# Dilated attention on one Trainium2 core: reordering softmax maxima and sums between token orders by VectorE transposes and quadrant copies instead of TensorE table products

## The chip, the cores and the metric

The kernel runs on one core of one Trainium2 chip. The metric is the device time of one execution in microseconds (us), as the median of several runs. Less is better.

## The reference

One decoder layer: a half-step feed-forward block, a mixer with two attention branches, and a second half-step feed-forward block, for 512 tokens and a model width of 1024. The change touches the dilated branch alone. It has three groups of eight heads; group 0 attends to a window of neighbours (stride 1), groups 1 and 2 to tokens 4 and 16 apart. The three groups of one head index are mixed by weights that come from their softmax maxima and sums:

```
m = jnp.max(logits, axis=-1, keepdims=True)
p = jnp.exp(logits - m)
den = jnp.sum(p, axis=-1, keepdims=True)
out = jnp.einsum('brnhqk,brnkhd->brnqhd', (p / den).astype(v.dtype), vv)
lse = (m + jnp.log(den))[..., 0]
...
w = jax.nn.softmax(jnp.stack(lses, axis=0), axis=0)
y = jnp.sum(w[..., None] * jnp.stack(outs, axis=0).astype(jnp.float32), axis=0)
```

For one token, `w` needs the maxima and sums of all three groups. Group 0 is computed with 128 consecutive tokens on the 128 partitions (token = 128b + p); groups 1 and 2 with every fourth token (token = 4p + b). So each group's maxima and sums must also be had in the other token order before the weights can be formed in both.

## The kernel before

All products are made on TensorE (PE) in three passes of high and low parts (`act_hi*w_hi`, `act_lo*w_hi`, `act_hi*w_lo`). The weights stream in as pieces: SyncE (SP) loads a piece into one of four `raw` buffers, ScalarE (ACT) rounds it to `w_hi` (`split_hi`), VectorE (DVE) subtracts to get `w_lo` (`split_lo`, semaphore `lo_ready`), and PE multiplies 24 matmuls per whole piece. Two buffers of `w_hi` and `w_lo` exist, so ACT splits a piece only once PE is done with the one two before.

The dilated part handles two heads of each group at a time: `dilated_pair`, four turns (the first written out, three in a loop). Each turn has pieces q = 0 to 11: q 0 to 5 give queries and keys of the three groups, 6 to 8 the values, 9 and the half pieces 10 and 11 two output gates. Each engine has its own program in written order and waits on semaphores:

- PE: `dil_project(q)`, with scores (`dil_score`) after pieces 2, 4 and 6, value transposes (`turn_dil_values`) after 7, 8 and 9, then transposes of the probabilities (`turn_dil`) and the products with values (`attend_dil`) in and between the half pieces. `turn_dil_values(2)` after piece 9 needs VectorE's taking of piece 8 (semaphore `chunk_taken`); `turn_dil(0)` needs the probabilities of group 0 scaled by their weights (`scale_probs(0)`, `dil_scaled`).
- VectorE: `split_lo` of the next piece, `dil_maxima` (after pieces 3, 5, 7), `take_projection` (multiplying PE's result by `rstd`), and at q = 9 `group_weights`, `scale_probs` and `gate_take`.
- ScalarE: `split_hi`, the exponentials, which leave each row's sum in `stats`, one small exponential in the middle of `group_weights`, and copies of transposed values and probabilities out of PSUM.

`stats` has 128 partitions x 2 (maxima, sums) x 3 groups x 2 token orders x 8. The other order is produced by PE: after `turn_dil_values(1)` it multiplies `stats` by 0/1 tables in `const` (`C_FOLD` and `C_EXPAND`, 512 columns each), four products each, into bank 7 (lines L827 and L830). `group_weights` on VectorE waits for them (`stats_moved`), masks the result with two more small tables (L1551) and adds up with twelve reductions (L1559, L1562).

Of the kernel before, what the change touches and what calls it, by code (L numbers as in the profile page):

```python
# [28 lines left out]
ALU = mybir.AluOpType  # L29
# [94 lines left out]
LATENTS = (KQ, KQ + 1, 0, 1, 2, None)  # L124


C_IDENT, C_ONES, C_EXPAND, C_FOLD = 0, P, 2 * P, 2 * P + SEQ
C_MOD = C_FOLD + SEQ
C_DIV = C_MOD + BLOCKS
C_CAUSAL = C_DIV + BLOCKS  # L130
C_FREQ = C_CAUSAL + P
C_TURN, C_PHASE, C_SIGN, C_EPS = C_FREQ + 1, C_FREQ + 2, C_FREQ + 3, C_FREQ + 4
C_END = C_FREQ + 5
# [26 lines left out]
def shape_constants():  # L160

    c = np.zeros((P, C_END), np.float32)
    p = np.arange(P)
    j = np.arange(SEQ)
    c[:, C_IDENT:C_IDENT + P] = np.eye(P)
    c[:, C_ONES:C_ONES + P] = 1.0

    c[:, C_EXPAND:C_EXPAND + SEQ] = p[:, None] == j[None, :] // 4
    c[:, C_MOD:C_MOD + BLOCKS] = p[:, None] % 4 == np.arange(4)

    c[:, C_FOLD:C_FOLD + SEQ] = p[:, None] == (4 * (j % P) + j // P)[None, :] % P
    c[:, C_DIV:C_DIV + BLOCKS] = p[:, None] // 32 == np.arange(4)
    c[:, C_CAUSAL:C_CAUSAL + P] = np.where(p[None, :] <= p[:, None], 0.0, NEG_INF)

    freq = 1.0 / ROPE_THETA ** (np.arange(0, QK_ROPE, 2, dtype=np.float32) / np.float32(QK_ROPE))
    for row in range(QK_NOPE, P):
        c[row, C_FREQ] = freq.astype(np.float32)[row % 16]
        cosine = row < QK_DIM
        c[row, C_TURN] = 0.25 if cosine else 0.0
        c[row, C_PHASE] = math.pi / 2 if cosine else 0.0  # L180
        c[row, C_SIGN] = -1.0 if QK_DIM <= row < QK_DIM + 16 else 1.0
    c[:, C_EPS] = EPS
    onehot = np.zeros((NUM_BUCKETS, T5_END), np.float32)
    mask = np.full((GROUP_HEADS, T5_END), NEG_INF, np.float32)
    for g, stride in enumerate(STRIDES):
        apart = (T5_LEN[g] + 1) // 2 + (P // 2 if g == 0 else 0) - 1 - np.arange(T5_LEN[g])
        unit = 4 if g == 2 else 1
        ok = (apart >= 0) & (apart <= P) & (apart % unit == 0)
        bucket = t5_bucket(np.maximum(apart, 0) // unit * stride)
        at = T5_AT[g] + np.arange(T5_LEN[g])  # L190
        onehot[bucket[ok], at[ok]] = 1.0
        mask[:, at[ok]] = 0.0
    return c, onehot, mask


def decoder_layer(nc, x_t, positions, rel_bias, gains_in, tables, onehot_in, mask_in, ffn, w_latent, w_lora_up,
# [19 lines left out]
    def sem(name):  # L216
        return ctx.enter_context(nc.semaphore(name))

    with ctx:
# [30 lines left out]

        exchanged = work[:, 3, 0:6 * 4 * 2 * BLOCKS]


        hid_hi = shared("hid_hi", [P, KF, SEQ], F32R)
# [79 lines left out]
        dil_scores, dil_taken = sem("dil_scores"), sem("dil_taken")  # L336
        dil_max, dil_exp, dil_scaled = sem("dil_max"), sem("dil_exp"), sem("dil_scaled")
        v_turned, v_taken = sem("v_turned"), sem("v_taken")
        stats_moved, weight_ready, weight_exp = sem("stats_moved"), sem("weight_ready"), sem("weight_exp")

        mixed_rounded, mixed_split = sem("mixed_rounded"), sem("mixed_split")
        merge_ready, merged_rounded, merged_split = sem("merge_ready"), sem("merged_rounded"), sem("merged_split")
# [151 lines left out]
        def _(pe):  # L494
# [283 lines left out]
            def dilated_pair(i, first=False):  # L778
# [43 lines left out]
                pe.wait_ge(chunk_taken, c + e + 8)  # L822
                turn_dil_values(1, i)

                pe.wait_ge(dil_exp, 24 * i + 24)
                for b in range(BLOCKS):
                    nc.tensor.matmul(bank[7][:, b * 16:(b + 1) * 16], const[:, C_FOLD + b * P:C_FOLD + (b + 1) * P],  # L827
                                     stats[:, :, 0, 0, :], start=True, stop=True, skip_group_check=True)
                for b in range(BLOCKS):
                    last = nc.tensor.matmul(bank[7][:, 64 + b * 32:96 + b * 32],  # L830
                                            const[:, C_EXPAND + b * P:C_EXPAND + (b + 1) * P],
                                            stats[:, :, 1:3, 1, :], start=True, stop=True, skip_group_check=True)
                last.then_inc(stats_moved, 1)
                dil_project(9)
                pe.wait_ge(chunk_taken, c + e + 9)
                turn_dil_values(2, i)
# [40 lines left out]
        def _(act):  # L877
# [209 lines left out]
            def dilated_pair(i, first=False):  # L1087
                s, d, c, e = PIECES["dil"], 12 * i, CHUNKS["dil"], 11 * i
                for q in range(10):
                    if q or not first:  # L1090
                        split_hi(act, s + q + 1, d, HALF if q == 9 else TILES)
                    if q == 0 and not first:

                        gate_tanh(c + e - 1, MLA_HEADS - 1 + 2 * i)
                    if q in (3, 5, 7):
                        dil_exponentials(q // 2 - 1, i)
                    if q in (7, 8):
                        take_dil_values(q - 7, i)

                act.wait_ge(weight_ready, i + 1)  # L1100
                nc.scalar.activation(weight[:, :, :], weight[:, :, :], ACT.Exp).then_inc(weight_exp, 1)
                take_dil_values(2, i)
                split_hi(act, s + 11, d, HALF)
                for unit in range(8):
                    take_dil_probs(unit, i)
                    if unit == 1:
                        gate_tanh(c + e + 9, MLA_HEADS + 2 * i)
                    if unit == 4:
                        split_hi(act, s + 12, d, TILES)
# [34 lines left out]
        def _(dve):  # L1144
# [3 lines left out]
            def one():  # L1148
                count["turn"] += 1
                return 1  # L1150

            def so_far():
                return count["before"] + count["turn"] + count["earlier"]
# [384 lines left out]
            def take_projection(out, s, d, parity):  # L1538
                dve.wait_ge(piece_done, s + d + 1)
                nc.vector.tensor_tensor(out, bank[parity][:, :], rstd[:, :], ALU.mult).then_inc(chunk_taken, 1)  # L1540

            def group_weights(i):

                dve.wait_ge(stats_moved, i + 1)
                moved = exchanged
                mod, div = const[:, C_MOD:C_MOD + BLOCKS], const[:, C_DIV:C_DIV + BLOCKS]

                for at, n, mask in ((0, 8, div), (64, 16, mod)):
                    size = n * 8
                    view = "p (r k e) -> p r k e"  # L1550
                    nc.vector.tensor_tensor(  # L1551
                        moved[:, at:at + size].rearrange(view, k=BLOCKS, e=2),
                        bank[7][:, at:at + size].rearrange(view, k=BLOCKS, e=2),
                        mask.rearrange("p (a k e) -> p a k e", a=1, e=1).to_broadcast([P, n, BLOCKS, 2]), ALU.mult).then_inc(own, one())
                dve.wait_ge(own, so_far())
                for t in range(2):
                    for e in range(2):
                        source = moved[:, 0:64].rearrange("p (a t k e) -> p t e a k", a=BLOCKS, t=2, e=2)[:, t, e]
                        nc.vector.tensor_reduce(stats[:, t, 0, 1, e:8:2], source, AX.X, ALU.add)  # L1559
                        for g in (1, 2):  # L1560
                            source = moved[:, 64:192].rearrange("p (b t g k e) -> p t g e b k", b=BLOCKS, t=2, g=2, e=2)
                            last = nc.vector.tensor_reduce(stats[:, t, g, 0, e:8:2], source[:, t, g - 1, e], AX.X, ALU.add)  # L1562
                last.then_inc(own, one())
                dve.wait_ge(own, so_far())
                maxima_of = stats[:, 0, :, :, :].rearrange("p g o n -> p g (o n)")
                sums_of = stats[:, 1, :, :, :].rearrange("p g o n -> p g (o n)")
# [4 lines left out]
                top = neg_top[:, :].rearrange("p (a n) -> p a n", a=1).to_broadcast([P, GROUPS, 4 * BLOCKS])  # L1571
                nc.vector.tensor_tensor(weight[:, :, :], top, maxima_of, ALU.subtract).then_inc(weight_ready, 1)
                dve.wait_ge(weight_exp, i + 1)
                parts = exchanged[:, 0:GROUPS * 4 * BLOCKS]
                nc.vector.tensor_tensor(parts.rearrange("p (g n) -> p g n", g=GROUPS), weight[:, :, :],
                                                    sums_of, ALU.mult).then_inc(own, one())
                dve.wait_ge(own, so_far())
# [18 lines left out]
            def dilated_pair(i, first=False):  # L1596
                s, d, c, e = PIECES["dil"], 12 * i, CHUNKS["dil"], 11 * i
                for q in range(12):
                    tiles = HALF if q in (9, 10) else TILES
                    if q or not first:  # L1600
                        split_lo(dve, s + q + 1, d, tiles)
                    if q in (3, 5, 7):
                        dil_maxima(q // 2 - 1, i)
                    if q < 6:
                        out = (dil_q, dil_k)[q % 2][:, q // 2, :]
                    else:
                        out = dil_vt[:, q % 2, :]
                    if q == 0 and not first:

                        take_mixed(PAIRS - 1 + i, PAIRS + 8 * i, bank[2][:, :])  # L1610
                    if q < 9:
                        take_projection(out, s + q, d, (c + q) % 2)
                    if q == 9:
                        group_weights(i)
                        scale_probs(0)
                        gate_take(s + d + 10, (c + 9) % 2, MLA_HEADS + 2 * i)
                        for g in (1, 2):
                            scale_probs(g)
                gate_take(s + d + 12, 4, MLA_HEADS + 2 * i + 1)
            dilated_pair(0, first=True)  # L1620
            with dve.Fori(1, PAIRS) as i:
                enter_loop(i - 1, 2 + 1 + 2 + 4)
                dilated_pair(i)
            leave_loop(PAIRS - 1)

# [122 lines left out]
```

## Time and profile before

| | us |
|---|---|
| median of 3 runs | 1312.73 |
| lowest and highest run | 1310.87, 1315.46 |
| the profiled execution's own time | 1314.23 |
| its span, first to last instruction | 1312.4 |

| engine | busy us | share of the span |
|---|---|---|
| PE matmul | 1290.6 | 98% |
| PE weight load | 1048.9 | 80% |
| DVE | 653.1 | 50% |
| ACT | 443.0 | 34% |
| POOL | 18.7 | 1% |

The mean granted TensorE clock is 0.996 of full speed. Matmuls are pipelined, so PE's busy time is a union of overlapping records; the distance between the starts of two matmuls says more of what one costs than its duration. The four turns of the dilated part lie at about 545 to 860 us.

### The profile page before, as it was taken

What the parts mean: (1) busy time and instruction counts of PE and PEld (TensorE: products, weight loads), DVE (VectorE), ACT (ScalarE), POOL (GpSimd) and SP (SyncE); (2) the same over time, 40 slices, a digit from 0 to 9 for tenths busy, and PEclk for the clock granted to TensorE, in tenths of its full rate; (3) what the DMA queues carried; (4) which work ended last, traced back from release to release, by engine and by line L of the source; (5) the groups of instructions that cost most, each with busy time, mean ns of one, the idle gap of its engine ahead of it and who ended that gap; (6) DMA issues with size and microseconds to landing.
All of it is one profiled execution on the core that took longest, in us unless ns stands there. A gap on an engine that the chain in (4) does not pass through costs nothing.

```text
span 1312.4 us, 16722 instructions
## 1 busy us (share of the span) xinstructions
PE 1290.6 (98%) x6054; PEld 1048.9 (80%) x6054; DVE 653.1 (50%) x943; ACT 443.0 (34%) x763; POOL 18.7 (1%) x36
## 2 busy tenths in 40 slices
PE   8999999999999999999999999999999999999997
PEld 6788888888887777788888878778888888888886
DVE  5644444433345777544554545576644444443322
ACT  5322222322232444343333334423432222222221
POOL 0000000000000001200000000000000000000000
PEclk9999999999999999999999999999999999999998
DMA  6242232233321112512222221123222222223331
GB/s 224 97 110 96 96 96 96 88 104 89 104 90 62 67 54 79 130 50 82 78 65 86 74 80 64 64 96 96 97 96 96 96 96 96 96 90 91 100 88 64
DMA packets 36066, 118.87 MB, mean 91 GB/s; under 512 B 4680, under 2 KB 4680, under 8 KB 36032
## 3 DMA queue, kind: packets, MB, share of 16 engines
q1 hardware_dynamic: 34416, 114.83, 27.2%
q0 software_dynamic: 1328, 3.56, 1.5%
q8 instruction: 20, 0.33, 0.1%
q14 instruction: 14, 0.11, 0.0%
q10 hardware_dynamic: 288, 0.03, 0.0%
HBM read 115.85 MB, written 2.55 MB: 90 GB/s over the span
## 4 chain that ended last, share of the span: by engine, by line
PE 93%; DVE 3%; ACT 1%; issue 1%; DMA 1%; SPq 0%; POOL 0%; POOLq 0%; ACTq 0%; DVEq 0%
PE bank L545 36%; PE bank L378 17%; PE bank L380 16%; PE bank L379 16%; PE bank L732 2%; PE bank L755 1%; PE bank L649 1%; ACT w_hi L360 1%; PE bank L676 1%; DVE mla_stats L1441 1%; PE bank L665 1%; PE bank L772 1%; PE bank L768 1%; PE bank L512 0%; PE bank L741 0%
## 5 line engine op out<-in xcount | busy, mean ns | idle before, releaser
L365 DVE TENSOR_TENSOR w_lo<-raw,w_hi 128x1024 fp32r<-128x1024 f32 (+2 forms) x221 | 259.1, 1172 | 252.9 <-ACT w_hi L360 251.2
L360 ACT ACTIVATE w_hi<-raw 128x1024 fp32r<-128x1024 f32 (+2 forms) x221 | 224.3, 1015 | 446.7 <-PE bank L545 230.4
L545 PE MATMUL bank<-act_hi,w_hi 128*128 128x512 f32 x704 | 218.4, 391 | 2.8 <-DVE act_lo L1165 2.8
L545 PE MATMUL bank<-act_lo,w_hi 128*128 128x512 f32 x704 | 216.8, 389 | 0.0
L545 PE MATMUL bank<-act_hi,w_lo 128*128 128x512 f32 x704 | 216.6, 389 | 0.0
L378 PE MATMUL bank<-act_hi,w_hi 128*128 128x512 f32 x528 | 212.7, 403 | 2.9 <-DVE mla_vt L1434 1.5
L380 PE MATMUL bank<-act_hi,w_lo 128*128 128x512 f32 x528 | 206.7, 391 | 0.0
L379 PE MATMUL bank<-act_lo,w_hi 128*128 128x512 f32 x528 | 206.5, 391 | 0.0
L545 PEld LDWEIGHTS bank<-act_hi,w_hi 128*128 128x128 f32 x704 | 132.1, 188 | 32.2 <-DVE w_lo L365 3.2
L545 PEld LDWEIGHTS bank<-act_lo,w_hi 128*128 128x128 f32 x704 | 132.1, 188 | 27.7
L545 PEld LDWEIGHTS bank<-act_hi,w_lo 128*128 128x128 f32 x704 | 132.1, 188 | 27.5
L378 PE MATMUL bank<-hid_hi,w_hi 128*128 128x512 f32 x352 | 136.9, 389 | 0.0
L379 PE MATMUL bank<-hid_lo,w_hi 128*128 128x512 f32 x352 | 136.9, 389 | 0.0
L380 PE MATMUL bank<-hid_hi,w_lo 128*128 128x512 f32 x352 | 136.9, 389 | 0.0
L378 PEld LDWEIGHTS bank<-act_hi,w_hi 128*128 128x128 f32 x528 | 99.5, 188 | 29.6 <-issue 6.5
L380 PEld LDWEIGHTS bank<-act_hi,w_lo 128*128 128x128 f32 x528 | 99.5, 188 | 21.8
L379 PEld LDWEIGHTS bank<-act_lo,w_hi 128*128 128x128 f32 x528 | 99.7, 189 | 18.7
L1250 DVE TENSOR_TENSOR work<-bank,rstd 128x512 f32<-128x512 f32 x44 | 30.4, 692 | 123.3 <-PE bank L545 123.2
L380 PEld LDWEIGHTS bank<-hid_hi,w_lo 128*128 128x128 f32 x352 | 66.1, 188 | 13.8
L379 PEld LDWEIGHTS bank<-hid_lo,w_hi 128*128 128x128 f32 x352 | 66.1, 188 | 13.7
L378 PEld LDWEIGHTS bank<-hid_hi,w_hi 128*128 128x128 f32 x352 | 66.1, 188 | 13.6
L925 ACT ACTIVATE hid_hi<-work 128x512 f32 (+1 forms) x44 | 27.8, 632 | 94.8 <-DVE work L1256 94.8
(173 smaller groups left out, 1070.1 us busy)
## 6 DMA issues: line engine op xcount, KB each, us to landing
raw<-in_ffn_up SPq DMA_DIRECT2D x87, 512.0 KB, 3.4
raw<-in_w_dil SPq DMA_DIRECT2D x40, 512.0 KB, 3.4
raw<-in_ffn_down SPq DMA_DIRECT2D x32, 448.0 KB, 3.3
raw<-in_ffn_down SPq DMA_DIRECT2D x16, 512.0 KB, 3.5
raw<-in_w_mla_gates SPq DMA_DIRECT2D x8, 512.0 KB, 3.5
raw<-in_w_branches SPq DMA_DIRECT2D x8, 512.0 KB, 3.4
raw<-in_w_out SPq DMA_DIRECT2D x8, 512.0 KB, 3.4
raw<-in_w_latent SPq DMA_DIRECT2D x6, 512.0 KB, 3.5
```

The costliest lines, as they stand in the source:

```text
L360: nc.scalar.activation(w_hi[:, s % SPLIT, 0:tiles * P], raw[:, s % RAW, 0:tiles * P], ACT.Copy).then_inc(hi_ready, 1)
L365: nc.vector.tensor_tensor(w_lo[:, s % SPLIT, 0:tiles * P], raw[:, s % RAW, 0:tiles * P], w_hi[:, s % SPLIT, 0:tiles * P].bitcast(F32), ALU ...
L378: nc.tensor.matmul(out, a, hi(k), start=first, stop=False)
L379: nc.tensor.matmul(out, a, lo(k), start=False, stop=False)
L380: last = nc.tensor.matmul(out, b, hi(k), start=False, stop=end)
L545: last = nc.tensor.matmul(out, w[:, s % SPLIT, tile * P:(tile + 1) * P], moving[:, row, :], start=row == 0 and w is w_hi and moving is act_hi,
L649: nc.tensor.matmul(out, mla_q[0:QK_DIM, h % 2, b * P:(b + 1) * P], mla_k[0:QK_DIM, h % 2, 0:(b + 1) * P], start=True, stop=False, skip_gro ...
L665: last = nc.tensor.transpose(bank[5 + unit % 2][:, at:at + P], mla_p[:, row * P:(row + 1) * P], ident)
L676: last = nc.tensor.matmul(bank[7][V_DIM * e:V_DIM * (e + 1), key * P:SEQ], mla_v[:, e, key, :], probs_t[:, e, at:at + width], start=key == ...
L732: last = nc.tensor.matmul(out, dil_q[rows, g, tokens(g, b)], dil_k[rows, g, keys], start=True, stop=True, skip_group_check=True)
L925: nc.scalar.activation(hid_hi[:, bass.ds(2 * i + 2 * turn + j, 1), :], work[:, 3:4, :], ACT.Copy).then_inc(hid_rounded, 1)
L1250: nc.vector.tensor_tensor(work[:, 0, :], bank[c % UP_BANKS][:, :], rstd[:, :], ALU.mult).then_inc(chunk_taken, 1)
```

## The change

The eight table products per turn, their tables and the masks and reductions behind them go. Two VectorE functions take their place. Both use that a 32x32 transpose works within blocks of 32 partitions, and that a copy may move data from one quadrant (32 partitions) to another:

- `fold_stats` (at q = 5) brings group 0's maxima and sums into the order of groups 1 and 2: a transpose, four copies that gather the quadrants, a transpose, four copies that spread them.
- `expand_stats` (at q = 8) brings groups 1 and 2 into group 0's order: eight copies, a transpose, four copies, a transpose.
- On VectorE `group_weights` and `scale_probs(0)` move from q = 9 to q = 8, ahead of the taking of piece 8. On ScalarE the small exponential moves ahead of the copy of the second values.
- The table that is loaded at the start has 389 columns in place of 1421.

```diff
-C_IDENT, C_ONES, C_EXPAND, C_FOLD = 0, P, 2 * P, 2 * P + SEQ
-C_MOD = C_FOLD + SEQ
-C_DIV = C_MOD + BLOCKS
-C_CAUSAL = C_DIV + BLOCKS
+C_IDENT, C_ONES, C_CAUSAL = 0, P, 2 * P
...
-                pe.wait_ge(dil_exp, 24 * i + 24)
-                for b in range(BLOCKS):
-                    nc.tensor.matmul(bank[7][:, b * 16:(b + 1) * 16], const[:, C_FOLD + b * P:C_FOLD + (b + 1) * P],
-                                     stats[:, :, 0, 0, :], start=True, stop=True, skip_group_check=True)
-                for b in range(BLOCKS):
-                    last = nc.tensor.matmul(bank[7][:, 64 + b * 32:96 + b * 32],
-                                            const[:, C_EXPAND + b * P:C_EXPAND + (b + 1) * P],
-                                            stats[:, :, 1:3, 1, :], start=True, stop=True, skip_group_check=True)
-                last.then_inc(stats_moved, 1)
                 dil_project(9)
...
+                    if q == 8:
+
+                        act.wait_ge(weight_ready, i + 1)
+                        nc.scalar.activation(weight[:, :, :], weight[:, :, :], ACT.Exp).then_inc(weight_exp, 1)
                     if q in (7, 8):
                         take_dil_values(q - 7, i)
 
-                act.wait_ge(weight_ready, i + 1)
-                nc.scalar.activation(weight[:, :, :], weight[:, :, :], ACT.Exp).then_inc(weight_exp, 1)
                 take_dil_values(2, i)
...
+            def fold_stats(i):
+
+                dve.wait_ge(dil_exp, 24 * i + 8)
+                dve.wait_ge(own, so_far())
+                nc.vector.transpose(squares, stats[:, :, 0, :, :].rearrange("p t o n -> p t (o n)")).then_inc(own, one())
+                dve.wait_ge(own, so_far())
+                for u in range(BLOCKS):
+                    last = nc.vector.tensor_copy(by_stat[:, :, 8 * u:8 * u + 8],
+                                                 squares[SQ * u:SQ * (u + 1), :].rearrange("i (q v) -> i v q", v=BLOCKS))
+                last.then_inc(own, one())
+                dve.wait_ge(own, so_far())
+                nc.vector.transpose(by_token, work[0:SQ, 3, 4 * SQ:8 * SQ]).then_inc(own, one())
+                dve.wait_ge(own, so_far())
+                for b in range(BLOCKS):
+                    source = by_token.rearrange("q (v t n) -> q t v n", v=BLOCKS, t=2)[:, :, :, 2 * b:2 * b + 2]
+                    last = nc.vector.tensor_copy(
+                        stats[SQ * b:SQ * (b + 1), :, 0, 1, :].rearrange("q t (v e) -> q t v e", e=2), source)
+                last.then_inc(own, one())
+
+            def expand_stats(i):
+
+                dve.wait_ge(dil_exp, 24 * i + 24)
+                dve.wait_ge(own, so_far())
+                for b in range(BLOCKS):
+                    for t in range(2):
+                        target = by_token.rearrange("q (v t g b e) -> q b t g v e", v=BLOCKS, b=BLOCKS, t=2, g=2)
+                        last = nc.vector.tensor_copy(
+                            target[:, b, t], stats[SQ * b:SQ * (b + 1), t, 1:3, 1, :].rearrange("q g (v e) -> q g v e", e=2))
+                last.then_inc(own, one())
+                dve.wait_ge(own, so_far())
+                nc.vector.transpose(work[0:SQ, 3, 4 * SQ:8 * SQ], by_token).then_inc(own, one())
+                dve.wait_ge(own, so_far())
+                for u in range(BLOCKS):
+                    last = nc.vector.tensor_copy(squares[SQ * u:SQ * (u + 1), :].rearrange("i (q v) -> i v q", v=BLOCKS),
+                                                 by_stat[:, :, 8 * u:8 * u + 8])
+                last.then_inc(own, one())
+                dve.wait_ge(own, so_far())
+                nc.vector.transpose(stats[:, :, 1:3, 0, :], squares).then_inc(own, one())
+
             def group_weights(i):
 
-                dve.wait_ge(stats_moved, i + 1)
...
                     tiles = HALF if q in (9, 10) else TILES
+                    if q == 8:
+                        expand_stats(i)
                     if q or not first:
                         split_lo(dve, s + q + 1, d, tiles)
                     if q in (3, 5, 7):
                         dil_maxima(q // 2 - 1, i)
+                    if q == 5:
+                        fold_stats(i)
+                    if q == 8:
+                        group_weights(i)
+                        scale_probs(0)
...
                     if q == 9:
-                        group_weights(i)
-                        scale_probs(0)
                         gate_take(s + d + 10, (c + 9) % 2, MLA_HEADS + 2 * i)
                         for g in (1, 2):
                             scale_probs(g)
                 gate_take(s + d + 12, 4, MLA_HEADS + 2 * i + 1)
+            nc.vector.memset(stats[:, :, 0, 1, :], 0.0).then_inc(own, one())
```

The place on PE is the seam between pieces 8 and 9 of the first turn. Before, PE's program reads there (L741 is the transpose of values, L827 and L830 the table products, L378 to L380 the three passes of a piece):

```order
L380 MATMUL bank<-act_hi,w_lo 128x512
L741 MATMUL bank<-const,dil_vt 128x128 [waits v_taken,chunk_taken]
L741 MATMUL bank<-const,dil_vt 128x128 x3
L827 MATMUL bank<-stats,const 128x16 [waits dil_exp]
L827 MATMUL bank<-stats,const 128x16 x3
L830 MATMUL bank<-stats,const 128x32 x4
L378 MATMUL bank<-act_hi,w_hi 128x512 [waits lo_ready,chunk_taken]
```

And with the change (line numbers are five lower):

```order
L375 MATMUL bank<-act_hi,w_lo 128x512
L736 MATMUL bank<-const,dil_vt 128x128 [waits v_taken,chunk_taken]
L736 MATMUL bank<-const,dil_vt 128x128 x3
L373 MATMUL bank<-act_hi,w_hi 128x512 [waits lo_ready,chunk_taken]
L374 MATMUL bank<-act_lo,w_hi 128x512
```

Eight products and a wait on `dil_exp` are gone; the first product of piece 9 follows the value transposes.

On VectorE the place is from the taking of piece 7 to the splitting of the half piece 10, in the first turn. Before (L1540 takes a piece, L365 is `split_lo`, L1551 masks):

```order
L1540 TENSOR_TENSOR dil_vt<-bank,rstd 128x512 [waits piece_done]
L365 TENSOR_TENSOR w_lo<-raw,w_hi 128x1024 [waits hi_ready]
L1540 TENSOR_TENSOR dil_vt<-bank,rstd 128x512 [waits piece_done]
L365 TENSOR_TENSOR w_lo<-raw,w_hi 128x512 [waits hi_ready]
L1551 TENSOR_TENSOR work<-bank,const 128x64 [waits stats_moved]
L1551 TENSOR_TENSOR work<-bank,const 128x128
L1559 TENSOR_REDUCE stats<-work 128x4 [waits own]
```

With the change, from the same taking of piece 7 (L1528) to the first instruction of `group_weights` (L1574):

```order
L1528 TENSOR_TENSOR dil_vt<-bank,rstd 128x512 [waits piece_done]
L1556 COPY work<-stats 32x2x4x2 [waits own,dil_exp]
L1556 COPY work<-stats 32x2x4x2 x7
L1560 STREAM_TRANSPOSE work<-work 32x128 [waits own]
L1563 COPY work<-work 32x4x8 [waits own]
L1563 COPY work<-work 32x4x8 x3
L1567 STREAM_TRANSPOSE stats<-work 128x2x2x8 [waits own]
L360 TENSOR_TENSOR w_lo<-raw,w_hi 128x1024 [waits hi_ready]
L1574 TENSOR_TENSOR neg_top<-stats 128x16 [waits own]
```

and further on, the end of `group_weights` (L1589), `scale_probs(0)` (L1599), and only then the taking of piece 8 and the splitting for piece 10:

```order
L1589 TENSOR_TENSOR weight<-weight,total 128x48 [waits own]
L1599 TENSOR_TENSOR dil_p<-dil_p,weight 128x128 [waits own]
L1599 TENSOR_TENSOR dil_p<-dil_p,weight 128x768
L1599 TENSOR_TENSOR dil_p<-dil_p,weight 128x128
L1599 TENSOR_TENSOR dil_p<-dil_p,weight 128x768
L1528 TENSOR_TENSOR dil_vt<-bank,rstd 128x512 [waits piece_done]
L360 TENSOR_TENSOR w_lo<-raw,w_hi 128x512 [waits hi_ready]
```

Fourteen small instructions now stand ahead of the splitting for piece 9, and the weights and the scaling of group 0 ahead of the taking of piece 8. `fold_stats` puts ten more at q = 5, between `dil_maxima(1)` and the taking of piece 5.

## Rows read from the trace of the kernel before

**Rows 1.** The page: busy time of PE, and the granted clock in 40 slices

```profile
PE 1290.6 (98%) x6054; PEld 1048.9 (80%) x6054; DVE 653.1 (50%) x943; ACT 443.0 (34%) x763; POOL 18.7 (1%) x36
...
PEclk9999999999999999999999999999999999999998
```

**Rows 2.** Waits of PE: us in total, times, longest us

```profile
PE bank L545 <- DVE act_lo L1165: 2.8, 1, 2.8
...
PE bank L772 <- ACT probs_t L1085: 1.3, 4, 0.3
```

**Rows 3.** PE's timeline, first turn, pieces 8 to 9: start us, length us

```profile
591.70 0.63 PE L741 MATMUL bank<-const,dil_vt 128*128 128x128 f32 x4
592.17 0.96 PE L827 MATMUL bank<-stats,const 128*128 128x16 f32 x8
592.99 1.06 PE L830 MATMUL bank<-stats,const 128*128 128x32 f32 x8
593.88 0.48 PE L378 MATMUL bank<-act_hi,w_hi 128*128 128x512 f32 x1
```

**Rows 4.** PE's timeline, first turn, pieces 7 to 8

```profile
585.77 0.60 PE L741 MATMUL bank<-const,dil_vt 128*128 128x128 f32 x4
586.12 0.48 PE L378 MATMUL bank<-act_hi,w_hi 128*128 128x512 f32 x1
```

**Rows 5.** The tile `stats`: the table products, count, ns, first and last start

```profile
L827 PE MATMUL bank<-stats,const x32: 182/262/263, 592.2 to 828.0; 128*128 128x16 f32 x32
```

**Rows 6.** PE's timeline, last turn, pieces 8 to 9

```profile
826.78 0.63 PE L741 MATMUL bank<-const,dil_vt 128*128 128x128 f32 x4
...
828.96 0.48 PE L378 MATMUL bank<-act_hi,w_hi 128*128 128x512 f32 x1
```

**Rows 7.** VectorE's timeline, first turn, q = 7 to 9

```profile
585.97 0.69 DVE L1540 TENSOR_TENSOR dil_vt<-bank,rstd 128x512 f32<-128x512 f32 x1 [2.83 <-PE bank L380]
587.98 1.23 DVE L365 TENSOR_TENSOR w_lo<-raw,w_hi 128x1024 fp32r<-128x1024 f32 x1 [1.32 <-ACT w_hi L360]
...
593.52 0.69 DVE L365 TENSOR_TENSOR w_lo<-raw,w_hi 128x512 fp32r<-128x512 f32 x1 [0.93 <-ACT w_hi L360]
...
595.28 0.16 DVE L1559 TENSOR_REDUCE stats<-work 128x4 f32<-128x16 f32 x1
595.36 0.23 DVE L1562 TENSOR_REDUCE stats<-work 128x4 f32<-128x16 f32 x2
595.63 0.17 DVE L1567 TENSOR_TENSOR neg_top<-stats 128x16 f32<-128x16 f32 x1
595.84 0.17 DVE L1569 TENSOR_TENSOR neg_top<-neg_top,stats 128x16 f32<-128x16 f32 x1
...
597.58 2.23 DVE L1593 TENSOR_TENSOR dil_p<-dil_p,weight 128x128 f32<-128x128 f32 x4
```

**Rows 8.** ScalarE's timeline, first turn, q = 7 to 9

```profile
584.86 0.19 ACT L1073 ACTIVATION_READ_ACCUMULATOR dil_p<-dil_p,stats 128x1 f32 x1
...
586.89 1.06 ACT L360 ACTIVATE w_hi<-raw 128x1024 fp32r<-128x1024 f32 x1
592.38 0.59 ACT L1078 COPY dil_v<-bank 128x512 f32<-128x512 f32 x1 [4.43 <-PE bank L741]
```

**Rows 9.** VectorE's timeline, first turn, q = 5

```profile
569.15 0.69 DVE L1534 TENSOR_REDUCE stats<-dil_p 128x4 f32<-128x512 f32 x1
572.68 0.69 DVE L1540 TENSOR_TENSOR dil_k<-bank,rstd 128x512 f32<-128x512 f32 x1 [2.84 <-PE bank L380]
```

**Rows 10.** PE's timeline, first turn, after piece 9

```profile
599.42 0.63 PE L741 MATMUL bank<-const,dil_vt 128*128 128x128 f32 x4
599.89 1.04 PE L755 MATMUL bank<-const,dil_p 128*128 128x128 f32 x8
```

**Rows 11.** Loads of the dilated pieces: count, KB each, median us to landing

```profile
raw<-in_w_dil SPq DMA_DIRECT2D x40, 512.0 KB, 3.4
```

**Rows 12.** PE's timeline at the start: the first product that uses the table

```profile
23.49 1.02 PE L504 MATMUL bank<-const,sumsq 128*128 128x1 f32 x8 [1.00 <-DVE sumsq L1324]
```

More of the change, by code:

```diff
@@ L163, in shape_constants @@
     p = np.arange(P)
-    j = np.arange(SEQ)
     c[:, C_IDENT:C_IDENT + P] = np.eye(P)
     c[:, C_ONES:C_ONES + P] = 1.0
[L168 to L172, printed above, removed]
     c[:, C_CAUSAL:C_CAUSAL + P] = np.where(p[None, :] <= p[:, None], 0.0, NEG_INF)
@@ L249, in decoder_layer @@
         causal = const[:, C_CAUSAL:C_CAUSAL + P]
-        exchanged = work[:, 3, 0:6 * 4 * 2 * BLOCKS]
+        SQ = 32
+        parts = work[:, 3, 0:GROUPS * 4 * BLOCKS]
+        squares = work[:, 3, 2 * SQ:3 * SQ]
+        by_stat = work[0:SQ, 3, 4 * SQ:8 * SQ].rearrange("i (v t) -> i v t", v=BLOCKS)
+        by_token = work[0:SQ, 3, 8 * SQ:12 * SQ]
         hid_hi = shared("hid_hi", [P, KF, SEQ], F32R)
@@ L338, in decoder_layer @@
         v_turned, v_taken = sem("v_turned"), sem("v_taken")
-        stats_moved, weight_ready, weight_exp = sem("stats_moved"), sem("weight_ready"), sem("weight_exp")
+        weight_ready, weight_exp = sem("weight_ready"), sem("weight_exp")
         mixed_rounded, mixed_split = sem("mixed_rounded"), sem("mixed_split")
@@ L1540, in take_projection @@
                 nc.vector.tensor_tensor(out, bank[parity][:, :], rstd[:, :], ALU.mult).then_inc(chunk_taken, 1)
-            def group_weights(i):
-                dve.wait_ge(stats_moved, i + 1)
[L1545 to L1563, printed above, removed]
@@ L1573, in group_weights @@
                 dve.wait_ge(weight_exp, i + 1)
-                parts = exchanged[:, 0:GROUPS * 4 * BLOCKS]
                 nc.vector.tensor_tensor(parts.rearrange("p (g n) -> p g n", g=GROUPS), weight[:, :, :],
@@ L1619, in dilated_pair @@
                 gate_take(s + d + 12, 4, MLA_HEADS + 2 * i + 1)
+            nc.vector.memset(stats[:, :, 0, 1, :], 0.0).then_inc(own, one())
             dilated_pair(0, first=True)
             with dve.Fori(1, PAIRS) as i:
-                enter_loop(i - 1, 2 + 1 + 2 + 4)
+                enter_loop(i - 1, 4 + 4 + 2 + 4)
                 dilated_pair(i)
```

## The prediction

> **What bounds the kernel now.** I read the page's engine shares first. PE's matmuls cover 98% of the span and the granted clock stays at nine tenths or more in all slices but the last, which stands at eight [rows 1], so the full level of 2.4 GHz holds throughout: this kernel is TensorE's program, laid end to end. Then I read PE's own waits, to see whether any large hole is left that another engine could fill or widen. There is none: the longest is 2.8 us once at the start, and in the dilated part there are four waits of 0.3 us for copies of probabilities [rows 2]. So time moves only if PE's own stream gets shorter, or if something it needs comes late. With VectorE at 50% of the span, its share alone says nothing on lateness; that is read from the timeline of one turn, at the instructions that PE waits for.
>
> **What is removed.** Between the value transposes of piece 8 and the first product of piece 9 PE issues the eight table products. From the start of the transposes to the start of piece 9 takes 593.88 - 591.70 = 2.18 us [rows 3]. The same seam one piece earlier, the same four transposes with nothing behind them, takes 586.12 - 585.77 = 0.35 us [rows 4]. The table products thus cost 1.83 us, although their outputs are only 16 and 32 columns wide: each appears as two records, 16 in all. They stand in the last turn as in the first, 828.96 - 826.78 = 2.18 us, and the 32 records of L827 make eight in each of four turns [rows 5, 6]. Four turns give 4 x 1.83 = 7.3 us. Nothing hides them: PE is in them without a break. A lower bound on the gain from this step alone would be nothing, if piece 9 could not start sooner; the next part checks that.
>
> **What piece 9 needs.** Up to the seam nothing moves on PE, so I keep the old times for it. Without the table products piece 9 would start at 591.70 + 0.36 = 592.06. It needs `w_lo` of piece 9, which was made from 587.98 to 589.21 [rows 7], and taking 7, done at 586.66. In the change `expand_stats` stands ahead of that splitting. It waits for the last exponential, which ends at 585.05 [rows 8], before VectorE is done with taking 7. So `expand_stats` may run from about 586.6, and the splitting (1.23 us) must start by 592.06 - 1.23 = 590.8. That leaves 4.2 us. The time the change gives to fourteen small instructions is what decides.
>
> **Price of expand_stats.** The trace has neither a transpose on VectorE nor a copy between quadrants. The nearest rows are operations of 16 elements per partition. Reductions without a wait between them last 0.16 and start 595.36 - 595.28 = 0.08 us apart [rows 7]. Dependent ones, each with a wait on the one before, start 595.84 - 595.63 = 0.21 us apart [rows 7]. All fourteen at the dependent pace make 2.9 us; the overlapping pace, ten steps of 0.08 and four dependent ones of 0.21, gives 10 x 0.08 + 4 x 0.21 = 1.6 us. The transpose of 32x128 has 128 elements per partition: between 0.69 us for 512 and 1.23 us for 1024 lies 1.05 ns per element [rows 7], so it adds about 0.12 us over a 16-element operation, and even as dear as a 512-wide one (0.69) it would add 0.5. The other transpose and the later copies are at 32 elements and add next to nothing. Ends: 1.7 and 2.9 + 2 x 0.5 = 3.9 us. I take 2.4, in the middle: the copies move between quadrants and I have no row on whether those overlap.
>
> On that point the Trainium skill speaks against the change: "VectorE: DVE Perf Modes", section "The DRAIN you can't avoid", says that the next operation does not start before the pipe of the one before is empty, and tells authors to keep the count of operations small; its section on two Vector instructions with no wait between them adds that an instruction whose input or output starts in another quadrant than the last one's is held until all earlier ones are done. The trace's 0.08 us step shows overlap within one quadrant; for these copies, which change quadrant, the page makes the dependent pace the right one. By the page the sum for `expand_stats` would be the 2.9 us above, by the overlapping rows 1.6.
>
> At 2.4 us it ends at 589.0, so the splitting starts 1.0 us later than before and ends at 590.2, 1.8 us before PE asks. Even 3.9 us stays inside 4.2. The ten instructions of `fold_stats` cost 2.1 us at the dependent pace, 0.1 to 1.0 more for the transposes. VectorE idles 2.84 us there ahead of taking 5 [rows 9]; and that taking is first needed by scores that come after piece 6, a whole piece (some 5.9 us) later. Cost nothing; without that idle time the following taking and splitting would come at most 0.3 us later, still ahead of PE.
>
> **The moved weights.** Behind the splitting come `group_weights` from its first minimum on, 597.58 - 595.63 = 1.95 us including ScalarE's small exponential, `scale_probs(0)` 2.23 us and taking 8 with 0.69 us [rows 7]. From 590.2 that gives 594.4 for the scaling and 595.1 for taking 8. ScalarE is free for the exponential from 587.95 to 592.38 [rows 8] and is asked at about 590.8. What is queued behind it there are the copy of the second values and the splitting for piece 10; they wait for PE anyway until 592.38. The deadlines: PE's third value transposes need taking 8 at 599.42 - 1.83 = 597.6, and the first transposes of probabilities need the scaling at 599.89 - 1.83 = 598.1 [rows 10]. Slack 2.5 and 3.7 us. In the old order the scaling ended at 597.58 + 2.23 = 599.8 and let PE through just in time; on the new one it is early, but there was no hole there, so nothing more is gained.
>
> The low part for piece 10 slides from 593.52 to about 595.2. It is needed behind those transposes, after 598.1, and SP's next load waits for it: a load lands 3.4 us after issue [rows 11], at about 599, and is split only after piece 11, which is later than piece 9's end at 597.6 by all of the two half pieces, and PE's work between them. The removed masks, reductions and the wait on `stats_moved` save VectorE 1.3 us at a place where nobody waits for it. The shorter table is loaded at the start, where the first product that uses it waited for VectorE's sum, not for the table [rows 12]: nothing. The one added memset stands in idle time.
>
> **The sum.** 1314.23 - 7.3 = 1306.9 us for an execution like the profiled one, whose own time lies 1.5 us above the median of the runs; against the median, 1312.73 - 7.3 = 1305.4 us, or 0.56% less.
>
> **Rivals.**
> A, VectorE becomes late and the kernel slower. The place is the splitting for piece 9 behind `expand_stats`. Above 4.2 us each further microsecond is a hole in PE, four times. It breaks even at 4.2 + 1.83 = 6.0 us and is slower by 0.3% above 7.0. If each of the fourteen were as dear as a full 512-wide operation, 0.69 us, they would take 9.7: 4 x (5.5 - 1.8) = 14.7 us, 1327. For it speaks that no row shows a transpose; against it, that operations of this width take 0.15 to 0.21. Chance 0.05.
> B, part of the gain is given back inside the turn. After piece 9 PE, ScalarE and VectorE hand transposed probabilities to one another with little room, shown by the four waits of 0.3 us [rows 2]; if taking 8 or the scaling falls behind by more than the slack, or the new order disturbs that part, a microsecond per turn is lost and 1309.4 results. Against it: all that part is anchored to the end of piece 9 and has the same order as before. Chance 0.10.
> C, the change does not shorten PE: the products were cover for something else that PE then waits for, such as `w_hi` and `w_lo` or a load. 1312.7. Against it: `w_lo` for piece 9 was ready 4.7 us ahead of use [rows 3, 7]. Chance 0.05.
>
> **How the numbers follow.** The forecast, PE shorter by the whole 7.3 us, has 0.80. A measurement of this kernel tells about 0.3%, 3.9 us, from no change. The forecast is faster by more than that; B and C fall within it (0.15); A is slower (0.05). The forecast's own range is 1303 to 1308, from the spread of the runs. To hold 8 in 10 I take 1302 to 1310, which reaches to B's 1309.4.
>
> **What would show it.** Right: between the second value transposes and piece 9's first product about 0.36 us in all four turns; PE's busy time lower by some 7 us; `expand_stats` in 1.7 to 3.9 us and no wait of PE for `w_lo`, `dil_vt` or `dil_p`. Wrong: a transpose of over a microsecond, or a PE wait on VectorE in front of piece 9 or of the third value transposes.

## The result, and the profile after

| | before | after |
|---|---|---|
| median us (9 runs each) | 1313.51 | 1307.16 |
| lowest, highest | 1310.87, 1315.46 | 1305.09, 1309.47 |
| span of the profiled execution | 1312.4 | 1305.5 |

The ratio is 0.995, with a 95% interval of 0.9941 to 0.9959: faster by 5.4 to 7.7 us. The spans differ by 6.9 us.

The page of the kernel after, its head and engine shares:

```profile
span 1305.5 us, 16661 instructions
...
PE 1283.3 (98%) x5990; PEld 1041.8 (80%) x5990; DVE 662.2 (51%) x984; ACT 442.9 (34%) x763; POOL 18.8 (1%) x36
```

Against [rows 1] PE has 64 matmul records less and 7.3 us less to do; VectorE has 41 instructions and 9 us more, and PE is still at 98%.

PE's timeline of the kernel after, the same seam of the first turn as [rows 3], and below it the one of the last turn as [rows 6]:

```profile
591.83 0.63 PE L736 MATMUL bank<-const,dil_vt 128*128 128x128 f32 x4
592.22 0.48 PE L373 MATMUL bank<-act_hi,w_hi 128*128 128x512 f32 x1
...
821.61 0.63 PE L736 MATMUL bank<-const,dil_vt 128*128 128x128 f32 x4
822.00 0.48 PE L373 MATMUL bank<-act_hi,w_hi 128*128 128x512 f32 x1
```

The seam is now 592.22 - 591.83 = 0.39 us in the first turn and 822.00 - 821.61 = 0.39 in the last, where it was 2.18; the trace has the same 0.39 in the two turns between. (The seam one piece earlier, 0.35 in [rows 4], is what the prediction took for it.) The difference is 1.79 us, four times 7.16. After piece 9 of the last turn the third value transposes, which answer to [rows 10], lead straight into the transposes of probabilities:

```profile
827.57 0.63 PE L736 MATMUL bank<-const,dil_vt 128*128 128x128 f32 x4
828.03 0.71 PE L750 MATMUL bank<-const,dil_p 128*128 128x128 f32 x5
```

No hole opened there either. The price of it is on VectorE, whose timeline from taking 7 to the low part of piece 10 answers to [rows 7]:

```profile
586.10 0.69 DVE L1528 TENSOR_TENSOR dil_vt<-bank,rstd 128x512 f32<-128x512 f32 x1 [2.83 <-PE bank L375]
586.70 1.00 DVE L1556 COPY work<-stats 32x16 f32<-32x16 f32 x8
587.74 0.30 DVE L1560 STREAM_TRANSPOSE work<-work 32x128 f32<-32x128 f32 x1
588.08 0.79 DVE L1563 COPY work<-work 32x32 f32<-32x32 f32 x4
588.90 0.21 DVE L1567 STREAM_TRANSPOSE stats<-work 128x32 f32<-128x32 f32 x1
589.03 1.18 DVE L360 TENSOR_TENSOR w_lo<-raw,w_hi 128x1024 fp32r<-128x1024 f32 x1
...
592.07 2.23 DVE L1599 TENSOR_TENSOR dil_p<-dil_p,weight 128x128 f32<-128x128 f32 x4
594.22 0.68 DVE L1528 TENSOR_TENSOR dil_vt<-bank,rstd 128x512 f32<-128x512 f32 x1
594.82 0.68 DVE L360 TENSOR_TENSOR w_lo<-raw,w_hi 128x512 fp32r<-128x512 f32 x1
```

`expand_stats` runs from 586.70 to 589.11, 2.4 us. The low part of piece 9 is done at 590.21, 2.0 us before PE asks at 592.22. Taking 8 is done at 594.90, where PE asks at 597.78.

The ten instructions of `fold_stats`, in the idle time that [rows 9] shows, leave 0.88 us of its 2.84:

```profile
569.88 0.20 DVE L1534 STREAM_TRANSPOSE work<-stats 128x32 f32<-128x32 f32 x1
570.12 0.75 DVE L1537 COPY work<-work 32x32 f32<-32x32 f32 x4
570.90 0.30 DVE L1541 STREAM_TRANSPOSE work<-work 32x128 f32<-32x128 f32 x1
571.23 0.70 DVE L1545 COPY stats<-work 32x16 f32<-32x16 f32 x4
572.81 0.69 DVE L1528 TENSOR_TENSOR dil_k<-bank,rstd 128x512 f32<-128x512 f32 x1 [0.88 <-PE bank L375]
```

PE's waits after are those of the kernel before at the same places, no new one among them. The one at the start is a little longer; it differs from execution to execution, 1.9 to 3.5 us over the profiles of all these runs.

```profile
PE bank L540 <- DVE act_lo L1153: 3.2, 1, 3.2
...
PE bank L767 <- ACT probs_t L1071: 1.3, 4, 0.4
```

### The profile page after: what moved, and what is told of

It reads as the page before. It is cut to its first block, busy times and chain, and to the rows that moved or that the text cites. A ratio compares the mean times of both kernels' runs of the same rounds, so it can differ in the third digit from the quotient of the medians.

```text
span 1305.5 us, 16661 instructions
## 1 busy us (share of the span) xinstructions
PE 1283.3 (98%) x5990; PEld 1041.8 (80%) x5990; DVE 662.2 (51%) x984; ACT 442.9 (34%) x763; POOL 18.8 (1%) x36
## 4 chain that ended last, share of the span: by engine, by line
PE 93%; DVE 3%; ACT 2%; issue 1%; DMA 1%; SPq 0%; POOL 0%; POOLq 0%; ACTq 0%; DVEq 0%
PE bank L540 36%; PE bank L373 17%; PE bank L375 16%; PE bank L374 16%; PE bank L727 2%; PE bank L750 1%; PE bank L644 1%; ACT w_hi L355 1%; PE bank L671 1%; DVE mla_stats L1429 1%; PE bank L660 1%; PE bank L767 1%; PE bank L763 1%; PE bank L507 1%; PE bank L736 0%
```

## The experiments

The theory is the prediction's: the gain is the TensorE time of the eight products, and what VectorE does in their place is free as long as the low part of piece 9 is in time. The rivals: the gain comes from the new order or the shorter table; VectorE's chain is already on the path. All edits are to the changed kernel. Ratios are to the kernel before.

Spans of one kernel differ by some 2 us at the start and end of an execution. A finer measure is a stretch of PE's timeline, from the value transposes after piece 7 of the first turn to the first product with `sumsq` behind the dilated part: 943.38 - 585.77 = 357.61 us before and 936.47 - 585.90 = 350.57 after, 7.04 less. It is called the long stretch below.

**The products put back, on constants.**

```diff
+                pe.wait_ge(dil_exp, 24 * i + 24)
+                for b in range(4):
+                    nc.tensor.matmul(bank[7][:, b * 16:(b + 1) * 16], ident, ones[:, 0:16],
+                                     start=True, stop=True, skip_group_check=True)
+                for b in range(4):
+                    nc.tensor.matmul(bank[7][:, 64 + b * 32:96 + b * 32], ident, ones[:, 0:32],
+                                     start=True, stop=True, skip_group_check=True)
                 dil_project(9)
```

> The changed kernel with eight products of the removed shapes (four of 16 and four of 32 columns, each 128x128 stationary) put back at the same seam on TensorE, their results used by nobody. Theory (the gain is the PE time of these products and nothing else): the seam from value transposes to piece 9 grows from 0.39 back to about 2.2 us, four times, the span from 1305.5 to about 1312.7, a ratio to before of 1.00. Rival (the gain comes from VectorE's new order or the shorter table): the span stays near 1305.5 to 1307.

Measured: median 1314.04 us, ratio 1.0009 (0.9999 to 1.0019), span 1311.4. PE's timeline at the seam:

```profile
590.64 0.63 PE L736 MATMUL bank<-const,dil_vt 128*128 128x128 f32 x4
591.12 0.96 PE L822 MATMUL bank<-const 128*128 128x16 f32 x8
591.93 1.06 PE L825 MATMUL bank<-const 128*128 128x32 f32 x8
592.82 0.48 PE L373 MATMUL bank<-act_hi,w_hi 128*128 128x512 f32 x1
```

The seam is 592.82 - 590.64 = 2.18 us, to the hundredth that of [rows 3] (2.17 or 2.18 in the other turns), and the whole gain is gone, with VectorE's new work and the short table in place. The long stretch is 357.60 us, as before. That rules out the rival.

**Half of them.** The same with `range(2)` in both loops.

> The changed kernel with four products at the seam (two of 16 and two of 32 columns), half of what was removed, results unused. Theory (each product costs its own time on TensorE, whatever its few columns): the seam from value transposes to piece 9 is midway between 0.39 and 2.2 us, about 1.3 us, and the span 3.6 us above the changed kernel's. Rival (a fixed cost for switching to such products makes most of it): the seam nearer 2 us.

Measured: one time, 1309.38 us, span 1307.6. The seam:

```profile
590.27 0.63 PE L736 MATMUL bank<-const,dil_vt 128*128 128x128 f32 x4
...
591.55 0.48 PE L373 MATMUL bank<-act_hi,w_hi 128*128 128x512 f32 x1
```

The seam is 1.28 us in each of the four turns, midway between 0.39 and 2.18: no fixed part, 0.22 us on average for a product of 16 or 32 columns. The span is 2.1 us over the changed kernel's and not the 3.6 expected; the seam, not the span, is the measure at this size, since the spans of the changed kernel itself differ by 1.9 us from one profile to the next (1305.5, and 1303.6 below), of which 585.90 - 584.04 = 1.86 lies ahead of the long stretch. The long stretch is 354.03 us, 3.5 over the changed kernel's, where 3.6 was expected.

**The old place on VectorE.**

```diff
-                    if q == 8:
-                        expand_stats(i)
...
-                    if q == 8:
-                        group_weights(i)
-                        scale_probs(0)
...
                     if q == 9:
+                        expand_stats(i)
+                        group_weights(i)
+                        scale_probs(0)
                         gate_take(s + d + 10, (c + 9) % 2, MLA_HEADS + 2 * i)
```

and the small exponential on ScalarE back behind the loop.

> The changed kernel with expand_stats, group_weights, scale_probs(0) and ScalarE's small exponential back at q = 9, where group_weights stood before. Theory: VectorE starts the expansion after the low part of piece 10, at about 594.2, so the scaling of the first head is done at about 599.7 and of the second at 600.8, while TensorE comes to the transposes of probabilities at 598.2: holes of about 2.1 to 2.6 us per turn, 8.5 to 10 us in all, span 1314 to 1315.5, which is more than the whole gain. Rival (the place in VectorE's program does not matter, PE has other slack): 1305.5.

Measured: median 1316.01 us, ratio 1.0025 (1.0015 to 1.0034), span 1314.0. PE's timeline after piece 9, and its waits in total:

```profile
595.88 0.63 PE L736 MATMUL bank<-const,dil_vt 128*128 128x128 f32 x4
598.06 0.63 PE L750 MATMUL bank<-const,dil_p 128*128 128x128 f32 x4 [1.54 <-DVE dil_p L1597]
599.13 0.87 PE L750 MATMUL bank<-const,dil_p 128*128 128x128 f32 x4 [0.44 <-DVE dil_p L1597]
```

```profile
PE bank L750 <- DVE dil_p L1597: 7.6, 8, 1.5
```

The holes are where they were expected, at the first and the second head. The waits come to 1.9 us per turn; the long stretch is 360.82 us, 10.3 over the changed kernel's, where 8.5 to 10 was expected. The same work in the same number of instructions, one piece later, makes the kernel slower than before. The removal is worth something only together with the move.

**VectorE made later by 1.5, 2.9 and 4.4 us.** In `expand_stats`, with 2, 4 and 6 idle additions:

```diff
                 nc.vector.transpose(stats[:, :, 1:3, 0, :], squares).then_inc(own, one())
+                for _ in range(2):
+                    dve.wait_ge(own, so_far())
+                    nc.vector.tensor_tensor(work[:, 2, :], work[:, 1, :], work[:, 1, :], ALU.add).then_inc(own, one())
...
```

> The changed kernel with two dependent idle additions of 128x512 (0.73 us each) behind the last transpose of expand_stats. Theory: the low part of piece 9 ends at 591.7 in place of 590.2 and TensorE asks for it at 592.2, so nothing moves: span 1305.5 within 0.5. Rival (VectorE's chain from taking 7 to scaling is already on the path): 1.46 us per turn, 1311.3.

> The same with six idle additions, 4.38 us. Theory: the low part of piece 9 ends at 594.6, 2.4 us after TensorE asks; four holes of 2.4 us in front of piece 9, span about 1315.0, slower than before. Rival (the margin is not the one at piece 9): no hole there, or holes in front of the third value transposes.

> The run with six idle additions, but with four (2.9 us). Theory: the low part of piece 9 is 0.9 us late, four holes of 0.9 us, 3.6 us over the changed kernel, span about 1308.5. The open point is the granted clock after a hole: with holes of 2.2 us it fell to its half in two of four turns; if holes of 0.9 us do that too, some 1.5 us more for each such turn.

| additions | added us | median | ratio and interval | PE's waits for `w_lo` of piece 9 | long stretch |
|---|---|---|---|---|---|
| 0 | 0 | 1307.16 | 0.995 (0.9941 to 0.9959) | none | 350.57 |
| 2 | 1.5 | 1306.15 | 0.9943 (0.9927 to 0.996) | none | 350.57 |
| 4 | 2.9 | 1310.28 | 0.9971 (0.996 to 0.9982) | 3.0 us in four | 354.63 |
| 6 | 4.4 | 1316.91 | 1.0026 (1.0016 to 1.0036) | 8.9 us in four | 363.43 |

The rows of waits with four additions, and then with six:

```profile
PE bank L373 <- DVE w_lo L360: 3.0, 4, 0.8
```

```profile
PE bank L373 <- DVE w_lo L360: 8.9, 4, 2.3
```

The kink lies where the prediction put the deadline: between 1.5 and 2.9 us of delay, 2.0 by the timeline of after. The holes place it more closely. With four additions the low part of piece 9 ends at 592.11 and PE starts on it 0.15 us later, in the first turn:

```profile
590.79 0.63 PE L736 MATMUL bank<-const,dil_vt 128*128 128x128 f32 x4
592.26 0.47 PE L373 MATMUL bank<-act_hi,w_hi 128*128 128x512 f32 x1 [0.83 <-DVE w_lo L360]
```

The seam is 1.47 us there, 1.08 over the 0.39 of the changed kernel, for 2.9 us of delay; so the first 1.8 to 1.9 us cost nothing. With six additions it is 2.92 us, 2.53 over, for 4.4, which gives the same. The rival that VectorE's chain already bounds the kernel is out. Six additions cost more than their holes, though, which is told below.

**The long table again.** The table gets 1032 unused columns.

```diff
-C_FREQ = C_CAUSAL + P
+C_FREQ = C_CAUSAL + P + 1032
```

> The changed kernel with its table padded by 1032 unused columns, so that the load at the start is as long as before. Theory: the first product that uses it waits for VectorE's sum and not for the table, so nothing moves, within 0.5 us. Rival (a part of the gain came from the shorter load): up to 1 us longer, seen as a wait of TensorE before the first table product.

Measured: median 1305.86 us, ratio 0.995 (0.9934 to 0.9967), span 1303.0. The changed kernel itself ran once more beside it:

> The changed kernel once more, as the measure for the others of this call. Ratio to before 0.994 to 0.996, span 1305 to 1306.

It gave a median of 1306.43 us, ratio 0.9951 (0.9937 to 0.9965), span 1303.6. The long table takes 7.3 us to land in place of 5.3, and PE waits for nothing ahead of the first product that uses it. The long stretch is 350.50 and 350.55 us. The table's length is worth nothing that can be told.

**Another quadrant with each copy.**

```diff
-                for b in range(BLOCKS):
-                    for t in range(2):
+                for t in range(2):
+                    for b in range(BLOCKS):
```

> The changed kernel with the two loops of the eight copies in expand_stats exchanged, so that each copy reads from another quadrant than the one before, in place of every second. Theory (a copy overlaps the one before only when it stays in its quadrant): eight steps of about 0.17 us, the eight copies take 1.3 us in place of 1.00, and the time stays, because VectorE's margin covers it. Rival (all small copies overlap alike, and only the count sets the time): 1.00 us again.

Measured: one time, 1307.46 us, span 1305.7. VectorE's timeline, the eight copies:

```profile
586.78 1.40 DVE L1556 COPY work<-stats 32x16 f32<-32x16 f32 x8
```

The eight copies take 1.40 us in place of 1.00. Two copies in one quadrant overlap, as this row of the kernel after shows, cut out at 587.0 us: two copies that last 0.16 each take 0.24 together.

```profile
586.95 0.24 DVE L1556 COPY work<-stats 32x16 f32<-32x16 f32 x2
```

In this run a cut from 586.95 to 587.15 gives 0.34, the two behind one another:

```profile
586.95 0.34 DVE L1556 COPY work<-stats 32x16 f32<-32x16 f32 x2
```

So the overlap depends on the quadrant, not on the count; VectorE's room covers the 0.4 us, and the long stretch stays at 350.47 us. The Trainium skill, "VectorE: DVE Perf Modes", section "Two Vector instructions with no wait between them", says just that, that an instruction starting in another quadrant is held; the trace agrees, with 0.17 to 0.18 us per step against 0.08. Its section "The DRAIN you can't avoid" first says that the next operation does not start until the pipe is empty, and then that one that is not held starts earlier; the 0.24 us for two copies is the second case.

**A step beyond.** The four waits of 0.3 us of [rows 2] are still there. Ahead of the copy that they wait for, ScalarE rounds a whole piece.

```diff
-                    if unit == 4:
+                    if unit == 5:
                         split_hi(act, s + 12, d, TILES)
```

> A step beyond the change: on ScalarE the rounding of piece 12 moves behind the copy of the sixth transposed probabilities, in place of ahead of it. Theory: the four waits of 0.3 us in front of TensorE's products L767 go, the low part for the next turn comes 0.4 us later and is still 2 us early: span about 1304.2, 1.3 us under the changed kernel. Rival (the rounding was in time only where it stood): a new wait in front of the next turn's first piece and no gain.

Measured: median 1303.46 us, ratio 0.9919 (0.9906 to 0.9933), span 1301.7. The row for L767 is gone from PE's waits and no row took its place. Ahead of its products in the first turn PE goes straight on:

```profile
605.60 0.39 PE L373 MATMUL bank<-act_hi,w_hi 128*128 128x512 f32 x1
...
606.39 1.09 PE L767 MATMUL bank<-probs_t,dil_v 128*64 128x128 f32 x16
```

where in the changed kernel it waits:

```profile
606.31 0.40 PE L373 MATMUL bank<-act_hi,w_hi 128*128 128x512 f32 x1
...
607.45 1.09 PE L767 MATMUL bank<-probs_t,dil_v 128*64 128x128 f32 x16 [0.28 <-ACT probs_t L1071]
```

From start to start that is 1.14 against 0.79 us, 0.35 less, 1.4 us over four turns. The long stretch is 348.88 us, 1.7 less than the changed kernel's 350.55, where 1.3 was expected. The medians differ by 3.0 us, clear of noise, since the intervals of the two ratios end at 0.9933 and begin at 0.9937. The spans differ by 1.9: this execution was 1.15 us later at the first turn (585.19 against 584.04), and at the end PE's last products (L507) took 2.05 us in place of 3.50, with a granted clock from 1290 to 1295 of 1.00 in place of 0.71. So 1.7 us is what the edit shows. It is the fastest of these kernels.

## Why the prediction was right

- **What is removed**: 1.83 us per turn, 7.3 in all, was forecast; the rows show 1.79 and 7.16. The seam without the products takes 0.39 us and not the 0.35 taken from the earlier seam (the prediction goes on with 0.36, which changes nothing). With the products back it is 2.18 us again. The median fell by 6.35 us in the first comparison and by 7.1 in the one beside the other experiments; both intervals hold 7.2. The long stretch fell by 7.04. The profiled execution was forecast at 1306.9 and took 1307.25. The median was forecast at 1305.4 and was 1307.16: 0.8 of these 1.8 us is that the median of before was 1313.51 over nine runs and not the 1312.73 of the first three.
- **What piece 9 needs**: `expand_stats` could take 4.2 us; it took the 2.4 that was chosen between 1.7 and 3.9. By the seams of the runs with delays PE starts to wait at 2.4 + 1.9 = 4.3 us, where 4.2 was forecast. Two small things that the forecast left out nearly cancel: the chain overlaps its neighbours (it starts 0.09 us before taking 7 ends, and the low part starts at 589.03, 0.08 before the last transpose ends), and PE starts 0.15 us behind the end of the low part and not with it.
- **The price of the unknown operations**: the transpose of 32x128 lasted 0.30 us, 0.13 over a 16-element operation against 0.12 estimated, and that of 128x32 0.21. That the 2.4 came out is partly luck: it was chosen as the middle of a range, for want of a row on quadrants. Every second of the eight copies stays in its quadrant and overlaps, and those that change quadrant do not. The prediction took the rule of the skill to hold for all of them and got 2.9; with four copies at 0.08 in place of 0.21 the same sum gives 2.4.
- **fold_stats**: at the dependent pace and with its transposes it was put at 2.2 to 3.1 us; it took 2.05 (569.88 to 571.93), inside the idle 2.84.
- **The moved weights**: taking 8 was forecast to be done at 595.1 and was at 594.9; PE's third transposes came at 597.8, forecast 597.6. Here the prediction fell short: it said that nothing more is gained by the early scaling, and did not say that the gain hangs on it. The old order shows that it does: by the medians it takes 8.9 us more, which is more than the gain.
- **What was saved on VectorE**: the masks and reductions of the old kernel took 1.4 us of its time by the trace of before, 594.21 to 595.63, and not 1.3. Nobody waits there.
- **The rivals**: A's mechanism is real, with its place right. Its break-even was put at 6.0 us of `expand_stats`. At 2.4 + 2.9 = 5.3 us the kernel was still faster, at 2.4 + 4.4 = 6.8 it was slower, by 0.26%, near the 0.3% that the prediction put at 7.0. That nearness is not the prediction's merit alone, since in some executions a fall of the clock was added to the holes, told below, and the prediction had no such term. B did not occur; its four waits stayed as they were, and could be removed by themselves. C is ruled out by the seam.
- **The table**: worth nothing, as forecast.

## What to carry to other kernels

In this kernel a TensorE product of 16 columns costs as much as one of 32, about 0.22 us, and nearly as much as a pass of 512 columns in a piece, 0.23 us from start to start. (Eight records of products with one column take 24.38 - 23.49 = 0.89 us too, of which the first start is in [rows 12].) Each of these product records has a record of a weight load beside it, and no run separates the two, so which of them sets the price stays open. On an engine that is 98% busy, eight tiny products are worth moving to an engine at half load even as twenty-four instructions there. Before moving work off the bounding engine, find the next thing that it asks of the receiving engine and count the room to that deadline; here 4.2 us of room for 2.4 us of work decided, and the same work one piece later made the kernel slower than it was. The engines' shares tell nothing of this, a turn's timeline tells all of it.

## What had not been expected of the hardware

A hole in TensorE's work can cost more than its length. With six additions the four holes of 2.2 to 2.3 us sum to 8.9, yet the long stretch is 12.9 us and the span of the profiled execution 12.5 us over the changed kernel's. From the value transposes ahead of piece 9 to those behind it, the four turns take 9.97, 10.03, 8.41 and 8.39 us, where the changed kernel takes 5.95 to 5.97. The late start of piece 9 is 2.4 to 2.5 us of that in every turn; the first two turns lose another 1.5 and 1.6. There the products start some 0.43 to 0.47 us apart in place of 0.23: in the first turn from 594.76 to 597.45, in the second, where piece 9 starts with steps of 0.23, from about 676.4 to 679.4. Shown are the first products of four successive groups of three in the first turn:

```profile
594.76 0.77 PE L373 MATMUL bank<-act_hi,w_hi 128*128 128x512 f32 x1 [2.29 <-DVE w_lo L360]
...
596.17 0.63 PE L373 MATMUL bank<-act_hi,w_hi 128*128 128x512 f32 x1
...
597.45 0.61 PE L373 MATMUL bank<-act_hi,w_hi 128*128 128x512 f32 x1
...
598.37 0.40 PE L373 MATMUL bank<-act_hi,w_hi 128*128 128x512 f32 x1
```

The granted clock in such stretches, from the view by windows (us, then each engine's busy time and instructions, the clock, the DMA share and GB/s), first behind the hole of the first turn, then behind that of the third:

```profile
594.70:598.30 3.60, 3.54 (x9) 2.85 (x10) 3.09 (x10) 1.25 (x3) 0.00 (x0) 0.55 0.47 146
756.30:759.90 3.60, 3.60 (x18) 2.93 (x17) 3.15 (x10) 1.25 (x3) 0.00 (x0) 1.00 0.44 146
```

0.55 is near the lower level of 1.2 GHz, 1.00 is 2.4. In the first and second turn the clock fell behind a hole of 2.2 to 2.3 us, in the third and fourth it did not, so a hole of this length makes it possible and not certain; why these two, no run here tells. The profiled execution is also the slowest of the ten of this kernel. Four of the ten have a mean granted clock of 0.996, that of the changed kernel, and spans of 1313.0 to 1314.3 us, 7.5 to 8.8 over its 1305.5: no more than the holes. The old order shows the fall in its first turn, behind holes of 1.5 and 0.4 us (0.53 from 599.6 to 603.0), and not in the other three (1.00). Behind the holes of 0.7 to 0.8 us with four additions the clock stays at 1.00 in all four turns.
